# A new order of the scan's first round and of the first feed-forward splits, with chunk decays folded into ScalarE's bias columns

## The chip, the cores and the metric

One core of one Trainium2 chip runs the whole program in one launch. The metric is the device time of that core in microseconds. The engines are TensorE (PE, matmuls; PEld are its weight loads), VectorE (DVE), ScalarE (ACT), GpSimd (POOL) and the queue of SyncE (SP), which only issues loads. They run side by side and are ordered by semaphores written out by hand.

## The reference, cut to what matters

Two blocks over 256 tokens (272 in the first, which puts 16 meta tokens ahead) of width 1024, batch 1, all in float32. Block one: gated convolution and stick-breaking attention, merged and projected, then a feed-forward:

```
u, g = split(xn @ w_up_gate);  u = causal_dwconv(u, conv_w_ffn)      # width 2816
ffn = (gelu(u) * g) @ w_down
```

Block two: a layer of two scans side by side, then an attention layer. The layer of the scans, with SSD over chunks of 128 tokens and GLA (8 heads, keys of 64, values of 128) over chunks of C = 64:

```
z, xbc, dt, q, k, v, gate_lr, g = split(h @ w_in)
xs, B, C = split(silu(causal_conv(xbc)))
y = ssd_chunked_scan(xs, dt, a, B, C, d_skip);     y = rms(y * silu(z))
gcs = cumsum(log_decay within a chunk);  ref = gcs[32];  g_last = gcs[63]
scores = (q * exp(gcs - ref)) @ (k * exp(ref - gcs)),   causal
chunk_kv = (k * exp(g_last - gcs)) @ v;  the state is carried from chunk to chunk
o = scores @ v + (q * exp(gcs)) @ state;   o = rms(o) * silu(g)
out = concat(y, o) @ w_out
```

## The kernel before, in words

**Weights.** The host lays all weight matrices out as one stream of chunks, [128, 1024] each, in the order in which TensorE uses them. SyncE loads a chunk into one of four raw buffers. To multiply float32 with three fast passes, each chunk is split: ScalarE writes the rounded high half (`split_hi`, L559, `weights_hi`) and VectorE the rest (`split_lo`, L1063, `weights_lo`). Both rings hold four chunks. `feed(tile)` on either engine splits the chunk that lies four chunks ahead of the tile's own, since the tile's last matmul is what frees the ring's place. A tile is named by its stage and number: fu and fg are the up and gate projections of the feed-forward; es, eb, ec, ex, ez, eg, eq, ek, ev are those of the scan layer (small, B, C, xs, z, g, q, k, v). `project` (L1749, L1752 for ev) runs a tile: 24 matmuls of 256 columns for one chunk, 48 for the two chunks of ev. It waits first for its bank of PSUM (the tile that used the bank before must have been taken, by `conv_in`, `z_half` and so on) and then for `lo_ready` of its chunk. For the ones that matter here: feeding fu1 makes fu3's weights, fg1 makes fg3's, fu2 makes fu4's, fg2 makes fg4's; feeding ez0 makes eg1's, eg0 makes ex3's, ex2 makes eq1's, ez1 makes ek1's, eg1 and ex3 make the two of ev1, ez2 makes eg3's. Tile fg3 uses the bank of fg1, so it waits for `ffn_out(1)`.

**The feed-forward.** For each of 22 tiles i, VectorE scales u (`ffn_up`, L1313), ScalarE makes the first tap of the convolution (`ffn_tap`, L746), VectorE the two others (`ffn_conv`, L1320, two instructions), ScalarE the gelu (`ffn_gelu`, L751), GpSimd scales it (`ffn_scale`, L443), VectorE multiplies with the gate tile (`ffn_out`, L1328), ScalarE and GpSimd split the result (`ffn_high`, L755, `ffn_low`).

**The scan layer.** Rounds p = 0 to 3 each do one pair of GLA heads and two pairs u = 2p, 2p+1 of SSD heads. TensorE's order, one round: eq, ek, ev (round 0 has them ahead of the loop), ez(u), eg(u), ex(u+2), ez(u+1), eg(u+1), ex(u+3), and between these tiles the small products: `turn_x` (L1989, a transposition of xs), `ssd_heads` (L1998), `turn_keys` (L2010, transposes the decayed keys into bank 6), `gla_scores` (L2019, bank 6), `gla_kv` (L2031), `gla_out` (L2041 and L2044, bank 6), `gla_sums` (L2050). `turn_keys(p)` may write bank 6 only when `gla_norm(p-1)` has read it (`gla_on`):

```
pe.wait_ge(S("gla_kl"), p + 1)
need(pe, "gla_on", p)
```

On VectorE: `gate_sum` (L1388) and `decay_sums` (L1400) make the cumulative log decays `gcs` of two pairs; `conv_in` (L1367), `conv_rest` (L1375, three instructions) and `z_full` (L1384) do the convolution and the silu of an ex tile; `z_half` (L1435) and `z_full` those of ez and eg; `ssd_args` (L1442), `ssd_weights` (L1394), `ssd_y` (L1447), `gate_y` (L1452) and `ssd_low` (L1456) belong to SSD; `gla_scores` (L1462), `gla_states` (L1469, L1472) and `gla_norm` (L1480, L1486) to GLA. In round 0 VectorE also multiplies e_k into `kb` (L1540, `gla_kl`) and `ka` (L1543).

On ScalarE: `decays(u)` (L857, L862), `half_tanh` (L811), `tap` (L786), `take_values` (L872), `take_keys` (L878), `ssd_high` (L883, L884), `gla_exps` (L892 to L896), `gla_squares` (L900), `gla_rms` (L908, L910, with a table load before it, L542, and another at the next tanh).

On GpSimd: `gla_args(p)` (L506, L508) subtracts the chunk's reference columns from gcs, into `ka` and `kb`; `gla_keys` (L484) and `gla_products` (L490, L494, L496) multiply the exponentials with keys and queries, the queries in four products of 64 partitions each; `ssd_weights` (L470) and `ssd_add` (L476).

The order on every engine is that of the code; an instruction that waits holds up all behind it on its engine.

## Time and profile before

| | us |
|---|---|
| median of 3 runs | 849.03 (848.57 to 850.56) |
| the profiled execution, its own time | 848.99 |
| its span, first to last instruction | 847.2 |
| TensorE busy in the span | 830.6 |
| VectorE, ScalarE, GpSimd busy | 620.8, 499.1, 132.7 |

The profile is of one execution. Busy times are sums over the span; all positions in time below count from the span's start. A timeline row gives start, duration, engine, line, operation, output and inputs, and the number of instructions merged; in brackets stands the idle time before it and what ended it. The feed-forward's tiles start at about 302, the scan layer at about 496 us, and its first round ends at about 552.

### The profile page before, as it was taken

To read this page: it belongs to the slowest core of one execution; us is meant where nothing else is said; L and a number is where in the kernel's file an instruction comes from. 1 tells how busy PE (TensorE), PEld (TensorE's weight loads), DVE (VectorE), ACT (ScalarE), POOL (GpSimd) and SP (SyncE) were. 2 spreads that over 40 slices of the span, in tenths; PEclk is the share of its full clock that TensorE was granted. 3 is DMA by queue.
4 is the path that set the end of the run, shared out by engine and by line. 5 is a ranking of instruction groups with operands and counts; after the bars stand their busy time and mean duration, and the time that the engine had idled before them with its cause. 6 is when DMAs were issued, how large, how long until landed. Compare 5 with 4: busy or idle time off the path is not lost.

```text
span 847.2 us, 16833 instructions
## 1 busy us (share of the span) xinstructions
PE 830.6 (98%) x6770; PEld 800.5 (94%) x6770; DVE 620.8 (73%) x1044; ACT 499.1 (59%) x842; POOL 132.7 (16%) x131
## 2 busy tenths in 40 slices
PE   8999999999999999999999999889999999999997
PEld 7999999999999999999999999779999999888896
DVE  6547888886666688667664488997887697568764
ACT  7346657555454576555554469668768555346655
POOL 1000000000000305433441100332534011000002
PEclk9999999999999999999999999999999999999999
DMA  8754434346555536656566535455454375554431
GB/s 326 233 153 139 152 106 173 127 137 179 183 188 186 173 106 191 201 177 186 189 197 196 180 100 171 142 170 167 150 167 157 112 231 183 186 169 141 126 101 50
DMA packets 39565, 139.81 MB, mean 165 GB/s; under 512 B 4400, under 2 KB 5056, under 8 KB 39360
## 3 DMA queue, kind: packets, MB, share of 16 engines
q1 hardware_dynamic: 37728, 135.78, 50.1%
q10 hardware_dynamic: 1760, 2.96, 1.1%
q8 instruction: 54, 0.88, 0.4%
q14 instruction: 23, 0.19, 0.1%
HBM read 137.65 MB, written 1.06 MB: 164 GB/s over the span
## 4 chain that ended last, share of the span: by engine, by line
PE 90%; DVE 5%; ACT 2%; DMA 1%; issue 1%; SPq 0%; DVEq 0%; ACTq 0%
PE ps L1749 71%; PE ps L1777 5%; PE ps L1752 5%; DVE weights_lo L1063 1%; PE ps L1870 1%; PE ps L1855 1%; PE ps L1884 1%; PE ps L2127 1%; PE ps L2145 1%; PE ps L1998 1%; DMA hidden<-xT_in 1%; PE ps L2135 1%; DVE arena L1375 1%; PE ps L2041 0%; PE ps L2050 0%
## 5 line engine op out<-in xcount | busy, mean ns | idle before, releaser
L1749 PE MATMUL ps<-x_hi,weights_hi 128*128 128x256 f32 (+3 forms) x1288 | 373.0, 290 | 5.4 <-DVE weights_lo L1063 3.0
L1063 DVE TENSOR_TENSOR weights_lo<-raw_weights,weights_hi 128x1024 fp32r<-128x1024 f32 x251 | 311.5, 1245 | 85.4 <-ACT weights_hi L559 85.3
L1749 PE MATMUL ps<-x_lo,weights_hi 128*128 128x256 f32 (+3 forms) x1288 | 363.8, 282 | 0.0
L1749 PE MATMUL ps<-x_hi,weights_lo 128*128 128x256 f32 (+3 forms) x1288 | 363.2, 282 | 0.0
L559 ACT ACTIVATE weights_hi<-raw_weights 128x1024 fp32r<-128x1024 f32 x251 | 263.8, 1053 | 152.8 <-PE ps L1749 62.2
L1749 PEld LDWEIGHTS ps<-x_hi,weights_hi 128*128 128x128 f32 x1288 | 242.9, 189 | 13.6 <-issue 10.9
L1749 PEld LDWEIGHTS ps<-x_lo,weights_hi 128*128 128x128 f32 x1288 | 242.9, 189 | 1.0 <-issue 0.7
L1749 PEld LDWEIGHTS ps<-x_hi,weights_lo 128*128 128x128 f32 x1288 | 243.4, 189 | 0.0
L1749 PE MATMUL ps<-y_hi,weights_hi 128*128 128x256 f32 (+1 forms) x488 | 137.7, 282 | 0.0
L1749 PE MATMUL ps<-y_lo,weights_hi 128*128 128x256 f32 (+1 forms) x488 | 137.4, 282 | 0.0
L1749 PE MATMUL ps<-y_hi,weights_lo 128*128 128x256 f32 (+1 forms) x488 | 137.1, 281 | 0.0
L435 POOL TENSOR_TENSOR arena<-arena 128x256 f32<-128x256 f32 (+1 forms) x24 | 25.9, 1078 | 494.8 <-ACT arena L708 328.2
L1749 PEld LDWEIGHTS ps<-y_hi,weights_hi 128*128 128x128 f32 x488 | 92.0, 189 | 0.3 <-issue 0.2
L1749 PEld LDWEIGHTS ps<-y_lo,weights_hi 128*128 128x128 f32 x488 | 91.9, 188 | 0.3 <-issue 0.2
L1749 PEld LDWEIGHTS ps<-y_hi,weights_lo 128*128 128x128 f32 x488 | 92.0, 189 | 0.0
L443 POOL TENSOR_TENSOR arena<-arena,rinv 128x256 f32<-128x256 f32 x22 | 32.9, 1496 | 81.6 <-ACT arena L751 81.4
L1752 PE MATMUL ps<-weights_hi,x_hi 128*128 128x256 f32 (+1 forms) x96 | 31.0, 323 | 0.0
L1752 PE MATMUL ps<-weights_lo,x_hi 128*128 128x256 f32 (+1 forms) x96 | 30.6, 319 | 0.0
L1752 PE MATMUL ps<-weights_hi,x_lo 128*128 128x256 f32 (+1 forms) x96 | 30.6, 318 | 0.0
L746 ACT ACTIVATE arena<-arena,params 128x256 f32<-128x256 f32 x22 | 11.1, 510 | 30.2 <-DVE arena L1313 30.2
L1313 DVE TENSOR_TENSOR arena<-ps,rinv 128x258 f32<-128x258 f32 x22 | 9.4, 428 | 25.1 <-PE ps L1749 24.5
L1320 DVE SCALAR_TENSOR_TENSOR arena<-arena,params 128x256 f32<-128x256 f32 x44 | 21.9, 498 | 4.2 <-ACT arena L746 1.0
(265 smaller groups left out, 1049.6 us busy)
## 6 DMA issues: line engine op xcount, KB each, us to landing
raw_weights<-weights_in SPq DMA_DIRECT2D x252, 512.0 KB, 3.7
arena<-decay_rows ACTq DMA_DIRECT2D x8, 256.0 KB, 3.6
masks<-masks_in SPq DMA_DIRECT2D x1, 1186.0 KB, 8.3
hidden<-xT_in SPq DMA_DIRECT2D x2, 272.0 KB, 4.1
hidden<-xT_in SPq DMA_DIRECT2D x1, 544.0 KB, 5.6
raw_weights<-weights_in SPq DMA_DIRECT2D x2, 256.0 KB, 4.0
gate_w<-gate_w_in ACTq DMA_DIRECT2D x1, 256.0 KB, 5.7
out<-arena ACTq DMA_DIRECT2D x1, 256.0 KB, 2.1
```

Source lines behind the costliest of these rows:

```text
L435: ins = nc.gpsimd.tensor_tensor(sq[:, 0, t0:T], sq[:, 0, t0:T], sq[:, i, t0:T], ALU.add)
L443: g.sig(nc.gpsimd.tensor_tensor(fgl[:, i % 2, :], fgl[:, i % 2, :], rinv[:, META:T], ALU.mult), "gelu_scaled")
L559: a.sig(A(whi[:, s * CW:(s + 1) * CW], raw[:, (c % RAW) * CW:(c % RAW + 1) * CW], ACT.Copy), "hi_ready")
L746: a.sig(A(fcv[:, i % 2, :], fu[:, i % 2, 0:L], ACT.Copy, scale=pcol("conv_ffn", i)), "tap_ready")
L1063: d.sig(TT(wlo[:, s * CW:(s + 1) * CW], raw[:, (c % RAW) * CW:(c % RAW + 1) * CW], whi[:, s * CW:(s + 1) * CW].bitcast(F32), ALU.subtract) ...
L1313: d.sig(TT(fu[:, i % 2, :], r, rinv[:, TA:T], ALU.mult), "u_ready")
L1320: ins = STT(out=c_, in0=u[:, j:L + j], scalar=pcol("conv_ffn", FT * j + i), in1=c_, op0=ALU.mult, op1=ALU.add)
L1375: ins = STT(out=dst, in0=scr2[:, n % 2, j:L + j], scalar=pcol("even_conv", 10 * j + ct), in1=dst, op0=ALU.mult, op1=ALU.add)
L1749: ins = mm(bank(BANK_OF[no])[:, 0:b - a], wt, x_[:, kt, a:b], start=s0, stop=s1)
L1752: ins = mm(bank(BANK_OF[no + o])[0:t1 - t0, 0:step * P], x_[:, kt, t0:t1], wt, start=s0, stop=s1)
L1777: ins = mm(bank(BANK_OF[no])[:, 0:b - a], w_[:, at:at + P], x_[:, kt, a:b], start=kt == 0 and n == 0 and len(passes) == 2, stop=kt == KT - ...
L1855: ins = mm(bank(4 + e)[:, c0:c0 + T - t0], keysT[rows, p, k0:k0 + P], qpair[rows, p % 2, t0:T], start=n == 0, stop=n == 2, skip_group_chec ...
```

## The change: what it does

1. **GLA decays.** `gla_args` is gone from GpSimd. `decay_sums(n)` on VectorE adds three small products that put -gcs[63]/16, -gcs[32]/16 and gcs[32]/16 of each chunk into a new tile `decay_cols` and signals `gla_bias`. ScalarE's `gla_exps(p)` now reads gcs itself and takes these as bias columns: 12 activations of 64 columns and one of 256, in place of four of 256.
2. **Round 0 and the head of round 1.** ScalarE, VectorE and TensorE get a written-out order. On TensorE, gla_scores(0) moves from behind ex3 to behind eq1, ssd_heads(1) and turn_keys(0) from ahead of ex3 to behind it, gla_kv(0) behind ek1, gla_out(0) behind ev1 and ssd_heads(2), gla_sums(0) behind ez2. On VectorE the feeds come earlier and `gate_y(0)`, `gate_y(1)`, `ssd_low(0)`, `ssd_low(1)` later. `HALF` numbers the tanh buffers in the new order. The first pair's four half-height query products stay on GpSimd, which now counts VectorE's earlier signals (`g.n.update`), so that its own waits are for its own instructions.
3. **Feed-forward.** VectorE splits the chunk of fu1 between `ffn_conv(0)` and `ffn_conv(1)`, that of fg1 ahead of `ffn_out(1)`, that of fu2 ahead of `ffn_conv(2)`; ScalarE splits that of fu2 ahead of `ffn_tap(2)`.

The stream of tiles, the banks and the rings are as before. The diff, cut to its core:

```diff
+        decay_cols = sb("decay_columns", 48)[:].rearrange("p (k i c) -> p k i c", k=3, i=4)
...
-        HALF = {t: n for n, t in enumerate((s_, i_) for s_, i_, b_, n_ in STREAM if s_ in ("eb", "ec", "ex", "ez", "eg"))}
+        FIRST_HALF = [("eb", 0), ("ec", 0), ("ex", 0), ("ex", 1), ("ex", 2), ("ez", 0), ("eg", 0), ("ex", 3), ("ez", 1),
+                      ("eg", 1)]
+        HALF = {t: n for n, t in enumerate(FIRST_HALF + [(s_, i_) for s_, i_, b_, n_ in STREAM
+                                                         if s_ in ("ex", "ez", "eg") and (s_, i_) not in FIRST_HALF])}
...
             pool.wait_ge(S("cb_taken"), 2)
+            g.n.update(gla_kl=1, m_ready=4)
+            pool.wait_ge(S("gla_exp"), 1)
+            gla_products(0)
+            for p in range(1, 4):
+                ssd_weights(2 * p)
+                gla_keys(p)
+                gla_products(p)
+                ssd_add(2 * p - 1)
+                ssd_weights(2 * p + 1)
+                ssd_add(2 * p)
...
             for i in range(2, FT):
-                ffn_tap(i)
+                if i > 2:
+                    ffn_tap(i)
                 feed(("fu", i))
+                if i == 2:
+                    ffn_tap(i)
                 ffn_gelu(i)
...
             def gla_exps(p):
-                act.wait_ge(S("gla_arg"), p + 1)
+                act.wait_ge(S("gla_bias"), p // 2 + 1)
                 need(act, "gla_qk", p)
+                need(act, "sc_ready", p - 1)
                 need(act, "st_ready", p - 1)
-                a.step(A(em, ka[:, k, :], ACT.Exp, scale=-1.0 / 16))
-                a.step(A(kb[:, k, :], kb[:, k, :], ACT.Exp, scale=-1.0 / 16))
-                a.settle()
-                a.step(A(ka[:, k, :], ka[:, k, :], ACT.Exp, scale=1.0 / 16))
+                for n, (dst, scale) in enumerate(((kb[:, k, :], 1.0 / 16), (ka[:, k, :], 1.0 / 16), (em, -1.0 / 16))):
+                    for c in range(4):
+                        w_ = slice(64 * c, 64 * c + 64)
+                        a.step(A(dst[:, w_], gcs[:, p, w_], ACT.Exp, scale=scale, bias=decay_cols[:, n, p, c:c + 1]))
...
             decays(0)
+            take_values(0)
+            feed(("ez", 0))
+            half_tanh(("ex", 1), xs[:, 1, :])
+            feed(("eg", 0))
+            decays(1)
+            feed(("ex", 2))
+            gla_exps(0)
+            feed(("ez", 1))
+            tap(("ex", 2), 2, xs[:, 2, :])
+            take_keys(0)
+            feed(("eg", 1))
+            half_tanh(("ex", 2), xs[:, 2, :])
+            feed(("ex", 3))
+            half_tanh(("ez", 0), zs[:, 0, :])
+            act.wait_ge(S("xsilu"), 5)
+            half_tanh(("eg", 0), gs[:, 0, :])
+            decays(2)
+            tap(("ex", 3), 3, xs[:, 3, :])
+            feed(("eq", 1))
+            for p in range(1, 4):
+                feed(("ek", p))
+                if p == 1:
+                    gla_exps(1)
+                    take_values(1)
+                    feed(("ev", 1))
+                    half_tanh(("ex", 3), xs[:, 3, :])
+                    gla_squares(0)
+                    half_tanh(("ez", 1), zs[:, 1, :])
+                    act.wait_ge(S("xsilu"), 6)
+                    half_tanh(("eg", 1), gs[:, 1, :])
+                    ssd_high(0)
+                    decays(3)
+                    ssd_high(1)
+                    gla_rms(0)
+                    feed(("ez", 2))
+                    half_tanh(("ez", 2), zs[:, 0, :])
...
             ffn_up(0)
             ffn_up(1)
             ffn_conv(0)
+            feed(("fu", 1))
             ffn_conv(1)
-            feed(("fu", 1))
             ffn_out(0)
+            feed(("fg", 1))
             ffn_out(1)
-            feed(("fg", 1))
             for i in range(2, FT):
                 ffn_up(i)
                 if i > 2:
                     feed(("fg", i - 1))
+                else:
+                    feed(("fu", i))
                 ffn_conv(i)
                 if i > 2:
                     ffn_out(i - 1)
-                feed(("fu", i))
+                    feed(("fu", i))
...
+                at = gcs[:, 2 * n:2 * n + 2, :].rearrange("p i (c t) -> p i c t", t=64)
+                for k, (t, scale) in enumerate(((63, -1.0 / 16), (32, -1.0 / 16), (32, 1.0 / 16))):
+                    ins = TS(decay_cols[:, k, 2 * n:2 * n + 2, :], at[:, :, :, t], scale, None, ALU.mult)
+                    d.sig(ins, "gla_bias") if k == 2 else d.step(ins)
...
+            ssd_args(0)
+            ssd_weights(0)
+            split_lo()
+            z_full(("ex", 1), xs[:, 1, :], name="xsilu")
+            z_half(("ez", 0), zs[:, 0, :])
+            feed(("ez", 0))
+            ssd_y(0)
+            gate_sum()
+            decay_sums(0)
+            feed(("eg", 0))
+            z_half(("eg", 0), gs[:, 0, :])
+            ssd_weights(1)
+            ssd_args(1)
+            conv_in(("ex", 2))
+            feed(("ex", 2))
+            first_products()
+            z_half(("ez", 1), zs[:, 1, :])
+            feed(("ez", 1))
+            conv_rest(("ex", 2), 2, xs[:, 2, :])
+            ssd_y(1)
+            z_half(("eg", 1), gs[:, 1, :])
+            gla_scores(0)
+            z_full(("ex", 2), xs[:, 2, :], name="xsilu")
+            feed(("eg", 1))
+            conv_in(("ex", 3))
+            ssd_args(2)
+            gla_states(0)
+            feed(("ex", 3))
+            for p in range(1, 4):
+                take_queries(p)
+                if p == 1:
+                    take_keys(1)
+                    gate_both(0)
+                    feed(("eq", 1))
+                    conv_rest(("ex", 3), 3, xs[:, 3, :])
+                    ssd_y(2)
+                    feed(("ek", 1))
+                    z_full(("ex", 3), xs[:, 3, :], name="xsilu")
+                    gate_both(1)
+                    feed(("ev", 1))
+                    z_half(("ez", 2), zs[:, 0, :])
+                    ssd_args(3)
+                    ssd_low(0)
+                    feed(("ez", 2))
+                    ssd_low(1)
+                    gla_norm(0)
...
+                if p == 1:
+                    project(("eq", 1), xhi, xlo, META, T)
+                    gla_scores(0)
+                    project(("ek", 1), xhi, xlo, META, T)
+                    turn_x(2)
+                    gla_kv(0)
+                    project(("ev", 1), xhi, xlo, META, T, toks=toksL)
+                    ssd_heads(2)
+                    gla_out(0)
...
                 project(("ez", u), xhi, xlo, META, T)
+                if p == 1:
+                    gla_sums(0)
...
                 project(("eg", u + 1), xhi, xlo, META, T)
-                if p == 0:
-                    turn_keys(0)
-                    ssd_heads(1)
-                else:
+                if p:
                     gla_scores(p)
                 if p < 3:
                     project(("ex", u + 3), xhi, xlo, META, T)
                 if p == 0:
-                    gla_scores(0)
+                    ssd_heads(1)
+                    turn_keys(0)
```

`first_products()` is the pair of products into `kb` and `ka` (after a wait for `gla_exp`), and `gate_both(u)` is z_full of ez(u), z_full of eg(u) and gate_y(u).

## Rows read from the trace of the kernel before

**Rows 1.** Part 1 of the page: busy us, share of the span, instructions.

```profile
PE 830.6 (98%) x6770; PEld 800.5 (94%) x6770; DVE 620.8 (73%) x1044; ACT 499.1 (59%) x842; POOL 132.7 (16%) x131
```

**Rows 2.** Table of stretches: busy us (instructions) of PE, PEld, DVE, ACT, POOL, clock, DMA.

```profile
532.00:570.50 38.50, 32.95 (x260) 29.75 (x258) 35.74 (x57) 23.54 (x47) 12.45 (x13) 0.96 0.48 152
```

**Rows 3.** Waits in 495 to 575 us: in total, times, longest.

```profile
PE ps L1749 <- DVE weights_lo L1063: 2.4, 1, 2.4
PE ps L2041 <- DVE arena L1472: 2.4, 1, 2.4
```

**Rows 4.** Table of stretches, TensorE alone: busy us (instructions), granted clock.

```profile
539.00:542.00 3.00, 0.48 (x3) 1.00 0.03 10
...
543.40:546.80 3.40, 3.40 (x18) 0.50 0.46 153
...
559.00:562.00 3.00, 0.60 (x5) 1.00 0.39 152
562.00:565.00 3.00, 3.00 (x28) 1.00 0.44 105
```

**Rows 5.** Timeline of TensorE, 576 to 577 us.

```profile
576.69 0.38 PE L2010 MATMUL ps<-masks,arena 128*128 128x128 f32 x2
```

**Rows 6.** Timeline of VectorE, first round.

```profile
534.21 1.22 DVE L1063 TENSOR_TENSOR weights_lo<-raw_weights,weights_hi 128x1024 fp32r<-128x1024 f32 x1
...
543.72 1.75 DVE L1063 TENSOR_TENSOR weights_lo<-raw_weights,weights_hi 128x1024 fp32r<-128x1024 f32 x1
...
549.97 1.53 DVE L1375 SCALAR_TENSOR_TENSOR arena<-arena,params 128x256 f32<-128x256 f32 x3
...
574.21 0.87 DVE L1480 SCALAR_TENSOR_TENSOR arena<-ps,params,arena 128x256 f32<-128x256 f32 x2
```

**Rows 7.** Timeline of ScalarE, round 1.

```profile
566.11 0.40 ACT L892 ACTIVATE arena<-arena 128x256 f32<-128x256 f32 x1
...
567.48 1.04 ACT L559 ACTIVATE weights_hi<-raw_weights 128x1024 fp32r<-128x1024 f32 x1
...
571.02 1.28 ACT L542 ACT_TABLE_LOAD   x1
572.31 0.69 ACT L908 ACTIVATE arena<-ps,masks 128x512 f32<-128x512 f32 x1
...
576.62 1.48 ACT L857 ACTIVATE arena<-arena,dt_and_cumsum 128x256 f32<-128x256 f32 x4
578.00 0.51 ACT L862 ACTIVATE arena<-arena 128x384 f32<-128x384 f32 x1
...
578.83 1.04 ACT L559 ACTIVATE weights_hi<-raw_weights 128x1024 fp32r<-128x1024 f32 x1
```

**Rows 8.** Groups by line and shape, ScalarE, 500 to 575 us: busy, mean ns.

```profile
L857 ACT ACTIVATE arena<-arena,dt_and_cumsum 128x256 f32<-128x256 f32 x6 | 3.0, 498 | 1.2 <-DMA arena<-decay_rows 1.2
...
L857 ACT ACTIVATE arena<-arena,dt_and_cumsum 128x128 f32<-128x128 f32 x6 | 2.3, 388 | 0.0
```

**Rows 9.** Timeline of GpSimd, first products.

```profile
543.58 0.80 POOL L494 TENSOR_TENSOR arena<-arena 64x256 f32<-64x256 f32 x1
544.46 1.60 POOL L496 TENSOR_TENSOR arena<-arena 64x256 f32<-64x256 f32 x1
```

**Rows 10.** Timeline of all engines, start of the feed-forward.

```profile
317.53 1.05 ACT L559 ACTIVATE weights_hi<-raw_weights 128x1024 fp32r<-128x1024 f32 x1
...
319.30 1.76 DVE L1063 TENSOR_TENSOR weights_lo<-raw_weights,weights_hi 128x1024 fp32r<-128x1024 f32 x1
...
321.20 0.35 PE L1749 MATMUL ps<-x_hi,weights_hi 128*128 128x258 f32 x1 [0.56 <-DVE weights_lo L1063]
...
324.15 0.28 PE L1749 MATMUL ps<-x_hi,weights_hi 128*128 128x256 f32 x1
...
327.53 1.22 DVE L1063 TENSOR_TENSOR weights_lo<-raw_weights,weights_hi 128x1024 fp32r<-128x1024 f32 x1
...
330.14 0.28 PE L1749 MATMUL ps<-x_hi,weights_hi 128*128 128x256 f32 x1
```

102 lines of the change are left out of this document (23 added, 79 removed).

## Prediction, made before the changed kernel was run

> **What bounds the kernel now.** I read the page's busy times first. TensorE is busy for 830.6 of 847.2 us, VectorE for 620.8 and ScalarE for 499.1 [rows 1]; so only time in which TensorE waits, or runs at a lower clock, can be won, some 16 us in all. The table of stretches then says where the edited scan stands: in 532.0 to 570.5 us TensorE is busy 32.95 of 38.5 us and VectorE 35.74 [rows 2]. There VectorE is the bound, not TensorE. The waits of that stretch name two stops of 2.4 us each: the first matmul of tile eg1 waits for `weights_lo` (L1063), and `gla_out(0)` (L2041) waits for the last carry of `gla_states(0)` (L1472) [rows 3]. The same table with TensorE alone shows a third loss: after the first stop the granted clock is 0.50 for 3.4 us (543.4 to 546.8) and 18 matmuls run in it, where 3.0 us at 1.00 hold 28 [rows 4]. At 0.118 us a matmul, 18 need 2.1 us; so 1.3 us are lost. After the second stop the clock stays at 1.00. These three, 2.4 + 2.4 + 1.3, and a few tenths at other edges make 7 us: the most that a new order of the first round can give. In the feed-forward only 0.56 us are idle, before fu3 at 321.20 [rows 10].
>
> **The feed-forward.** VectorE now splits the fu1 chunk (feeding tile fu3) between the two first convolutions. ScalarE's high half comes at 318.6 (317.53 + 1.05), GpSimd is still idle, so VectorE is done at 318.6 + 1.2 = 319.8; today it ends at 319.30 + 1.76 = 321.06 [rows 10]. fu3 then follows fu2 without a wait: 0.7 us won (idle and the pipeline's fill). But work queues behind it. `ffn_conv(1)` ends at 321.35 (2 x 0.5, and GpSimd's first scale holds the port for 0.6). ScalarE stands in `ffn_gelu(1)` until then, so its high half of fg1 is ready at 321.8 + 1.0 = 322.7, and VectorE's low half at 324.0; `ffn_out(1)`, now behind it, ends at 324.3 and frees fg3's bank: fg3 starts at 324.45, where it starts at 324.15 now. Then `ffn_up(2)` 324.8, high half of fu2 325.7 (behind `ffn_high(1)`), low half 326.95, and only then `ffn_conv(2)` to 328.0, gelu 328.4, high half of fg2 329.4, low half 330.65. Today that low half starts at 327.53 and ends at 328.75, and tile fg4 starts at 330.14 with 1.4 us to spare [rows 10]. With the change fg4 starts at 330.75, 0.6 late, and fg5 waits up to 0.4 more for `ffn_out(3)`. After that VectorE has about 0.9 us a tile to spare and catches up, while TensorE, which has no idle time there, gives nothing back. I take +0.8 us; bounds -0.7 (nothing but the gain) and +1.3.
>
> **The scan up to the second tile of round 1.** VectorE's pieces: a low half takes 1.22 us (1.13 to the next start), a three-step convolution 1.53 [rows 6]. With `z_full(ex1)` ahead of `z_half(ez0)`, and feed(ez0) ahead of gate_sum, the low half for eg1 is ready at 537.4, not 541.9; eg1 starts at 539.1, right after turn_x(1), and the stop and the low clock there are gone. gate_sum, two scans, a settle and three tiny TENSOR_SCALARs end at 540.7 (no 128x8 row exists; 128x4 and 128x50 ones take 0.17 and 0.18, 0.1 apart, so 0.3 for three).
>
> The exponentials then cost more on ScalarE. Today four take 566.11 to 567.48, 1.37 us [rows 7]. Now twelve of 64 columns with a bias column, and one of 256, are issued. With a bias column, two of 256 columns and two of 128 take 1.38 us from 576.62 to the next start [rows 7]; their durations differ by 0.11 [rows 8], so they cost 0.40 and 0.29 each. The 0.11 for 128 columns makes 0.235 for 64: 12 x 0.235 + 0.32 = 3.1 us, 1.8 more per pair (bounds 0.1 each, 1.5 in all, and 0.29 each, 3.8). In return GpSimd loses its two subtractions per pair. The Trainium skill, "ScalarE: Activation LUTs", section "What ACT_TABLE_LOAD costs", gives 280 ns + 0.833 ns a column with a pointer bias and 93 ns of overlap; by it the twelve would make 2.9 us, an estimate.
>
> So `gla_exp` comes at 544.0 (541.9 today). GpSimd's four half-height products are the ones it does today; one takes 0.80 us with the port nearly free and 1.60 behind a VectorE pass, and the pass beside them takes 1.75 instead of 1.22 [rows 6, 9]. Letting the two alternate (operands in PSUM don't collide), they end at 548.8, VectorE's product for `gla_kl` at 547.0 and `ka` at 548.4. turn_keys(0) waits 0.9 us for the former; behind it queue eq1 (547.3), gla_scores(0) and ek1 (550.9). turn_x(2) and gla_kv(0) follow at 553.8, ev1 at 555.2 (behind `conv_in(ex3)`, which frees its bank), to 561.1. The states are ready at 556.4, so gla_out(0), now behind ssd_heads(2), waits for nothing. ez2 runs 563.5 to 566.4, then gla_sums(0), turn_x(3), and eg2 to 570.3. In the trace eg2's end is turn_keys(1) at 576.69 [rows 5]. The lead is 6.4 us.
>
> **What is late next: turn_keys(1).** It overwrites bank 6 and so waits for `gla_norm(0)` (`gla_on`). Today that sits at 574.21 and is done at 575.1, 1.6 us ahead of its reader [rows 5, 6]. In the new order more stands before it on both engines. ScalarE: gla_exps(1) 558.5 to 561.6, take_values(1) 562.3, two high halves 564.2, tanh ex3, squares, tanh ez1 565.3, wait for `xsilu` 6 at 566.1 (VectorE's convolution and feed alternate with GpSimd's six products of pair 1), tanh eg1 566.5, ssd_high(0) 0.8, decays(3) 2.2 (576.62 to 578.83 in the trace), ssd_high(1) 0.8, table load 1.3, Ln and Exp 1.3: 573.0 [rows 7]. Then feed(ez2) is ahead of gla_norm(0) on VectorE: high half 1.05, low half 1.15, ssd_low(1) 0.4, gla_norm 0.9: `gla_on` at 576.5, turn_keys(1) at 576.6. Against 576.69: -0.1 us. The whole lead becomes one wait of about 6.2 us. Bounds: VectorE's own work cannot bring it before 573.6 (-3.1, ScalarE never late); the dearer activation, twice in this chain, makes it 577.9 (+1.2).
>
> The row puts a table load at 1.29 us to the next start (571.02 to 572.31) [rows 7]. The same section of the Trainium skill's "ScalarE: Activation LUTs" adds a drain of 1.38 us to each load; by it turn_keys(1) would come at about 577.9, an estimate. The trace shows only some 0.1 us of it, and the sum goes by the trace.
>
> **The clock.** An idle stretch of 2.4 us, with little else around it, was followed by 3.4 us at 0.50; the other 2.4 us stop was not [rows 4]. A wait of 6.2 us is far beyond both, so I expect the lower level (1.2 GHz) when ex4 starts. One such stretch costs 1.3 us, two in a row 2.6; I take 1.7 (bounds 0 and 2.6). The Trainium skill, "TensorE: Matmul & The Clock Gate", section "What's actually happening", says the same of an idle array: its clock is halved until work comes; the trace agrees (0.50).
>
> Later rounds: pairs 2 and 3 pay 1.8 us more of ScalarE before gla_norm(p-1), which has 1.5 us of slack, but GpSimd starts its decay products earlier without gla_args, and that returns about a microsecond. I cost it at 0.1, and it goes into the rounding.
>
> **The sum**, against the profiled execution, 848.99 us around a span of 847.2 (median of the runs 849.03, the same): +0.8 - 0.1 + 1.7 = +2.4, so 851.4 us.
>
> **Rivals.**
> - *The wait stands, the clock holds.* For it: one of two stops left the clock alone. Against: this one is 2.6 times as long. 848.99 + 0.8 - 0.1 = 849.7. Chance 0.10.
> - *The ScalarE chain is shorter than I make it*, and turn_keys(1) is bound by VectorE alone near 574: the gain of 3.1 stays, the clock hardly falls, 846.7 (with the feed-forward's gain too 845.2). For it: VectorE has idle time in my walk only while it waits for ScalarE's high half of ez2. Against: six steps of this chain are priced by rows. Chance 0.14, 0.09 of it below 846.5.
> - *Slower: the 64-column activations cost what 128 columns cost*, 0.29 each. Then turn_keys(1) is at 577.9, the wait 7.5 us, and the clock stays low for two stretches: 848.99 + 0.8 + 1.2 + 2.6 = 853.6. It decides from 0.25 us an activation on. Chance 0.14.
>
> **Chances and range.** The forecast itself, 849.8 to 853.0, has 0.62. Within 0.3% (2.5 us, about what this measurement can tell from no change) means 846.5 to 851.6; the forecast lies at its upper edge and gives 0.28 above it. Slower: 0.28 + 0.13 = 0.41; faster 0.09; same 0.50. The range that leaves 2 in 10 out is 847.4 to 853.3.
>
> **What would show it.** Right: no wait at eg1 or at gla_out(0); low halves ready before fu3 but fg4 some 0.6 us late; eg2 ending near 570; then a wait of 5 to 7 us at turn_keys(1) (L2010 of before) ended by VectorE's gla_norm, and granted clock 0.50 behind it. Wrong: turn_keys(1) before 575, or a granted clock of 1.00 after it, or 64-column activations outside 0.19 to 0.29 us, or TensorE idle elsewhere in round 1.

## The result, and the profile after

The changed kernel takes 851.01 us (median of 18 runs, 850.07 to 852.00); the kernel before, on the same chip, 849.33 us (18 runs, 848.57 to 851.15). The recorded ratio is 1.0013, 95% interval 1.0007 to 1.0019: 0.13% slower, within the 0.3% that was called no change (the medians alone differ by 1.68 us, 0.20%). The profiled execution took 850.85 us around a span of 849.2, where before's took 848.99 around 847.2. Before's 18 runs on this chip fall into two groups with nothing between 849.49 and 850.26 us: ten around 849.0 and eight around 850.5. Its profile is one of the lower group. So the difference of the two profiles, 1.86 us, is near the largest that the runs show; counted from the upper group the change costs 0.5 us.

Part 1 of the page of the changed kernel, against [rows 1]: ScalarE works 6.4 us more, GpSimd 7.9 us less, TensorE 1.6 us more although its 6770 instructions are the same.

```profile
PE 832.2 (98%) x6770; PEld 802.0 (94%) x6770; DVE 621.9 (73%) x1050; ACT 505.5 (60%) x878; POOL 124.8 (15%) x123
```

The scan starts 0.7 us later than before, so the stretch that answers to [rows 2] is 532.7 to 571.2 us. In the table of stretches TensorE is busy for 37.02 us of 38.5 (32.95 before), at clock 1.00 (0.96 before), and does 309 matmuls (260 before):

```profile
532.70:571.20 38.50, 37.02 (x309) 34.21 (x307) 36.70 (x60) 30.78 (x74) 13.78 (x13) 1.00 0.57 168
```

So round 0 became what it was to become. The waits in 532 to 577 us, TensorE's lines, against [rows 3]: the two stops of 2.4 us are gone and one of 5.4 us has come.

```profile
PE ps L2059 <- DVE arena L1494: 5.4, 1, 5.4
...
PE ps L2059 <- DVE arena L1525: 0.6, 1, 0.6
```

L2059 is `turn_keys`, L1494 `gla_norm`; the 0.6 us are turn_keys(0)'s, for which 0.9 were forecast. TensorE's timeline (against [rows 5], 576.69) and the table of stretches with TensorE alone (against [rows 4]) show the wait and what follows it: 5.3 us without a matmul, then 4.8 us at clock 0.50 with 23 matmuls, then 31 matmuls in 3.4 us at 1.00. The mean of 0.81 over the wait means that the last 2.0 us of it were at 0.50 already, so the low level lasted 6.8 us in all.

```profile
575.95 0.66 PE L2059 MATMUL ps<-masks,arena 128*128 128x128 f32 x2 [5.37 <-DVE arena L1494]
```

```profile
570.60:575.90 5.30, 0.00 (x0) 0.81 0.63 209
575.90:580.70 4.80, 4.75 (x23) 0.50 0.52 170
580.70:584.10 3.40, 3.40 (x31) 1.00 0.12 48
```

The chain that ends in L1494, on ScalarE and then VectorE (timelines of both, against [rows 6, 7]). Four decay activations and two exponentials of decays(3) stand in it, then the table load, Ln, Exp and a high half; on VectorE the low half of that chunk and `ssd_low(1)` are still ahead of `gla_norm(0)`.

```profile
565.71 0.42 ACT L799 ACTIVATE arena<-arena 128x256 f32<-128x256 f32 x1 [0.16 <-DVE arena L1394]
...
566.74 1.48 ACT L845 ACTIVATE arena<-arena,dt_and_cumsum 128x256 f32<-128x256 f32 x4
...
569.77 1.28 ACT L527 ACT_TABLE_LOAD   x1
571.07 0.69 ACT L897 ACTIVATE arena<-ps,masks 128x512 f32<-128x512 f32 x1
...
572.33 1.04 ACT L544 ACTIVATE weights_hi<-raw_weights 128x1024 fp32r<-128x1024 f32 x1
```

```profile
573.40 1.23 DVE L1071 TENSOR_TENSOR weights_lo<-raw_weights,weights_hi 128x1024 fp32r<-128x1024 f32 x1 [0.81 <-ACT weights_hi L544]
574.54 0.48 DVE L1470 SCALAR_TENSOR_TENSOR y_lo<-arena,params,y_hi 128x256 fp32r<-128x256 f32 x1
574.93 0.87 DVE L1494 SCALAR_TENSOR_TENSOR arena<-ps,params,arena 128x256 f32<-128x256 f32 x2
```

In the feed-forward the waits in 300 to 340 us answer to [rows 10]. The first is that ahead of fg3 (for `ffn_out(1)`, L1336), the second that ahead of fg4 (for its low half, L1071); the 0.56 us ahead of fu3 are gone.

```profile
PE ps L1798 <- DVE arena L1336: 0.8, 1, 0.8
PE ps L1798 <- DVE weights_lo L1071: 0.6, 1, 0.6
```

Round 3 has a loss that the prediction had put at 0.1 us and rounded away. ScalarE does its twelve exponentials (2.97 us) ahead of the two high halves of ev3; VectorE stands 2.24 us for those, so `ssd_y(6)` (L1461) comes at 645.03, and turn_x(7) on TensorE waits 0.39 us for it (timelines of the three engines):

```profile
637.47 2.97 ACT L884 ACTIVATE arena<-arena,decay_columns 128x64 f32<-128x64 f32 x12
...
640.65 1.99 ACT L544 ACTIVATE weights_hi<-raw_weights 128x1024 fp32r<-128x1024 f32 x2
...
641.73 3.39 DVE L1071 TENSOR_TENSOR weights_lo<-raw_weights,weights_hi 128x1024 fp32r<-128x1024 f32 x2 [2.24 <-ACT weights_hi L544]
645.03 0.47 DVE L1461 SCALAR_TENSOR_TENSOR arena<-arena,params,ps 128x256 f32<-128x256 f32 x1
...
645.65 0.41 PE L2038 MATMUL ps<-masks,arena 128*128 128x128 f32 x2 [0.39 <-DVE arena L1461]
```

To compare kernels whose lines and clocks of start differ, I take differences between the starts of the same matmuls in each profiled timeline: F is the feed-forward's first matmul to the scan section's first; the others count from the latter, to turn_keys(1), turn_x(5), turn_x(7) and the first matmul of the output projection. What follows that is 186.1 us in all of them. What stands ahead of F differs by up to 1.4 us between the profiled executions (the first matmul of F comes at 301.72 to 303.13) and is no part of any edit. The latest of them is that of early states, the one profile in which the granted clock fell back to 0.50 early in the kernel (10.9 to 14.3 us), so its own time says nothing about its edit. A difference in F below 0.3 us says nothing either: the eight kernels with the change's lines in the feed-forward have 194.45 to 194.75.

| us | F | keys(1) | x(5) | x(7) | output |
|---|---|---|---|---|---|
| before | 193.74 | 80.84 | 113.06 | 148.06 | 159.43 |
| changed | 194.75 | 79.38 | 113.51 | 149.08 | 160.61 |
| old feed-forward order | 193.75 | 79.36 | 112.81 | 148.38 | 159.92 |
| feed-forward part alone | 194.74 | 82.40 | 114.59 | 149.60 | 160.92 |
| work in the wait | 194.71 | 79.38 | 111.38 | 146.95 | 158.48 |
| early normalisation | 194.71 | 74.94 | 111.01 | 146.61 | 158.14 |
| high halves first | 193.36 | 79.41 | 112.81 | 148.38 | 159.95 |
| early states | 194.53 | 74.97 | 111.06 | 146.62 | 158.14 |
| round 3 | 194.45 | 79.40 | 113.47 | 148.49 | 162.82 |
| four moves | 193.43 | 74.95 | 111.08 | 146.14 | 160.43 |
| exponentials ahead | 194.69 | 74.94 | 108.75 | 143.85 | 155.36 |
| the same, high halves first | 193.44 | 75.00 | 108.80 | 143.90 | 155.42 |
| decay columns alone | 193.69 | 81.64 | 115.19 | 150.43 | 161.92 |
| products on VectorE | 194.51 | 79.37 | 113.00 | 148.57 | 160.10 |

The first two rows are the whole account: +1.01 in the feed-forward; -1.46 up to turn_keys(1); +1.91 from there to turn_x(5), which holds the low clock; +0.57 from turn_x(5) to turn_x(7); +0.16 after; -0.29 ahead of F, which no edit touches. Together +1.90, and the last matmul of the changed kernel ends 1.90 us later (843.32 for 841.42).

### The profile page after: what moved, and what is told of

Read it like the earlier page. It is cut to its first block, busy times and chain, and to the rows that moved or that the text cites. A ratio compares the mean times of both kernels' runs of the same rounds, so it can differ in the third digit from the quotient of the medians.

```text
span 849.2 us, 16867 instructions
## 1 busy us (share of the span) xinstructions
PE 832.2 (98%) x6770; PEld 802.0 (94%) x6770; DVE 621.9 (73%) x1050; ACT 505.5 (60%) x878; POOL 124.8 (15%) x123
## 4 chain that ended last, share of the span: by engine, by line
PE 86%; DVE 6%; ACT 4%; issue 2%; DMA 1%; POOL 0%; SPq 0%; DVEq 0%; ACTq 0%; POOLq 0%
PE ps L1798 69%; PE ps L1826 5%; PE ps L1801 4%; DVE weights_lo L1071 2%; ACT weights_hi L544 1%; PE ps L1919 1%; PE ps L1904 1%; PE ps L1933 1%; PE ps L2185 1%; PE ps L2203 1%; DVE arena L1385 1%; DMA hidden<-xT_in 1%; PE ps L2193 1%; PE ps L2047 0%; ACT arena L845 0%
## 5 line engine op out<-in xcount | busy, mean ns | idle before, releaser
L1071 DVE TENSOR_TENSOR weights_lo<-raw_weights,weights_hi 128x1024 fp32r<-128x1024 f32 x251 | 311.9, 1247 | 91.4 <-ACT weights_hi L544 91.3
```

The costliest lines, as they stand in the source:

```text
L1071: d.sig(TT(wlo[:, s * CW:(s + 1) * CW], raw[:, (c % RAW) * CW:(c % RAW + 1) * CW], whi[:, s * CW:(s + 1) * CW].bitcast(F32), ALU.subtract) ...
```

## The experiments

Each ratio is the recorded one, to runs of the kernel before on the same chip. The medians of before were 850.29 us (35 runs) for experiments 1 to 4, 849.94 (29) for 5 to 8 and 850.47 (21) for 9 to 12, so a time below must not be set against the 849.33 above. No kernel here differs from before by as much as 2%; the intervals say which differences are clear of noise.

**1. Old feed-forward order.** The changed kernel, with before's place for the fu1 and fg1 low halves on VectorE and the tap of round 2 on ScalarE.

```
-            feed(("fu", 1))
             ffn_conv(1)
+            feed(("fu", 1))
             ffn_out(0)
-            feed(("fg", 1))
             ffn_out(1)
+            feed(("fg", 1))
```

> The changed kernel with the feed-forward's splits put back into the old order; the scan keeps the change. My theory: the feed-forward part costs 1.0 us (fg4 starts late and nothing gives it back), so this comes out 1.0 us below the changed kernel, about +0.5 us against the kernel before; the stretch from the first feed-forward tile to the first scan tile is 193.7 us again (194.75 in the changed kernel). Rival: the feed-forward part is hidden or neutral and all of the difference is the scan's; then this equals the changed kernel, +1.5 us.

849.68 us (11 runs), ratio to before 0.9997 (0.9988 to 1.0005), the same as before within the interval. F goes back to 193.75 from 194.75.

**2. The feed-forward part alone.** The same lines the other way round, in the kernel before.

> The kernel before with only the feed-forward part of the change. My theory: +1.0 us against the kernel before (850.3), tile fu3 starting without a wait and fg4 and fg5 late. Rival, that the earlier split pays as it is meant to: -0.7 us (848.6).

851.36 us (12 runs), ratio 1.0011 (1.0002 to 1.0020). F is 194.74: the edit costs 1.00 us wherever it stands. That the two experiments agree to 0.01 is partly luck: over all profiles with these lines F is 0.7 to 1.0 us above before's. But this scan, which is before's to the letter, is 1.5 us longer. Both stops of 2.4 us are there as in [rows 3]; this time the granted clock also fell behind the second. The table of stretches has 19 matmuls in 3.7 us where [rows 4] have 28 in 3.0:

```profile
562.60:566.30 3.70, 3.70 (x19) 0.54 0.42 130
```

So whether a 2.4 us stop costs clock differs between executions of one order, and 1.5 us of a single profile's difference can be that. The runs of the kernel before say the same. For 85 of them the mean granted clock is on record. Of the 45 with 0.996 or more, 34 took 849.51 us or less; the 40 with 0.995 or less took 849.94 or more, all of them. The two groups of the result lie at the same times; their clocks are not on record.

**3. Work in the wait.** The changed kernel, with nine matmuls into the unused sums bank ahead of turn_keys(1); nothing reads them. The timeline has them as 18 instructions, 4.05 us together.

```
             def turn_keys(p):
+                if p == 1:
+                    for _ in range(9):
+                        mm(bank(SSB)[:, 0:L], ones, mask("ones"), start=True, stop=True)
                 pe.wait_ge(S("gla_kl"), p + 1)
```

> The changed kernel with nine matmuls of the ones mask (0.54 us each by the five that the kernel already uses this way) put into the wait at turn_keys(1), writing a bank nobody reads. My theory: the clock's fall is a cost of its own; the granted clock stays at 1.00 behind the wait, ex4 and ez3 take 5.8 us and not 7.8, and the kernel is 2.1 us below the changed one, about -0.5 us against the kernel before. Rival, that the low clock is hidden because VectorE and ScalarE bound that stretch anyway: the same as the changed kernel, or slower by what the matmuls push turn_keys(1) back (under 0.3 us).

849.10 us (11 runs), ratio 0.9991 (0.9983 to 1.0000). Its table of stretches, TensorE alone:

```profile
571.00:576.50 5.50, 4.05 (x20) 1.00 0.69 212
576.50:580.50 4.00, 3.96 (x34) 1.00 0.49 138
```

turn_keys(1) comes at the same time (79.38), but the clock stays at 1.00, and turn_x(5) is at 111.38 instead of 113.51: the low clock cost 2.13 us. In experiment 1, whose scan has the same order and the same wait of 5.4 us, the low stretch was 3.4 us instead of 6.8 and turn_x(5) at 112.81: 1.43 us. Its table of stretches, TensorE alone:

```profile
575.20:578.40 3.20, 3.16 (x15) 0.50 0.41 150
```

So the rival, a low clock hidden behind VectorE and ScalarE, falls.

**4. Early normalisation.** The two moves that put the chain to gla_norm(0) ahead of work that nobody waits for.

```
                     half_tanh(("eg", 1), gs[:, 1, :])
+                    gla_rms(0)
                     ssd_high(0)
                     decays(3)
                     ssd_high(1)
-                    gla_rms(0)
...
                     feed(("ev", 1))
+                    gla_norm(0)
                     z_half(("ez", 2), zs[:, 0, :])
...
                     ssd_low(1)
-                    gla_norm(0)
```

> The changed kernel with gla_rms(0) moved ahead of ssd_high(0), decays(3), ssd_high(1) on ScalarE, and gla_norm(0) ahead of z_half(ez2), ssd_args(3), ssd_low and feed(ez2) on VectorE. My theory: the lead of the new first round is real and is swallowed by that chain alone; turn_keys(1) comes 4.2 us earlier, the wait before it falls to about 1.1 us, the clock stays at 1.00: 6 us below the changed kernel, about -4.5 us against the kernel before. Rival: another wait stands right behind (decay weights for ssd_heads(3), the split chunk of eg3) and takes the time back: within 1 us of the changed kernel.

849.26 us (12 runs), ratio 0.9991 (0.9981 to 1.0001). turn_keys(1) comes 4.44 us earlier (74.94) and the clock stays at 1.00, worth 2.13 more by experiment 3; yet at turn_x(5) only 2.50 us are left of the 6.57. The 6 us that I had expected were wrong; the rival, another wait right behind, was right in kind, though the wait is at neither of the two places that it names and a part of the gain stayed. TensorE's waits in 566 to 612 us, and VectorE's timeline:

```profile
PE ps L2090 <- DVE arena L1486: 3.2, 1, 3.2
PE ps L2059 <- DVE arena L1494: 0.9, 1, 0.9
PE ps L2038 <- DVE arena L1461: 0.5, 1, 0.5
```

```profile
591.67 1.27 DVE L1410 TENSOR_TENSOR_SCAN arena<-masks,arena 128x256 f32<-128x256 f32 x2
592.97 0.32 DVE L1414 TENSOR_SCALAR decay_columns<-arena 128x8 f32<-128x8 f32 x3
593.40 0.42 DVE L1377 TENSOR_TENSOR arena<-ps,rinv 128x256 f32<-128x256 f32 x1
...
594.05 0.73 DVE L1486 SCALAR_TENSOR_TENSOR arena<-arena,ps 128x128 f32<-128x128 f32 x2
```

gla_out(1) (L2090) now waits 3.2 us for gla_states(1) (L1486), which stands behind decay_sums(1) (L1410, L1414) and the start of ex5's convolution. In the changed kernel TensorE got there at 598.1 us, after the states (ready at 596.7), and no wait showed.

**5. High halves first.** The changed kernel, with ScalarE's high halves of the fg1 and fg2 chunks ahead of the gelus of tiles 1 and 2.

```
             ffn_gelu(0)
-            ffn_gelu(1)
             feed(("fg", 1))
+            ffn_gelu(1)
...
                     ffn_tap(i)
+                    feed(("fg", i))
                 ffn_gelu(i)
                 if i > 2:
                     ffn_high(i - 1)
-                feed(("fg", i))
+                    feed(("fg", i))
```

> The change with one more move in the feed-forward: ScalarE's high halves of the fg1 and fg2 chunks come ahead of gelu(1) and gelu(2). Theory (the queue behind the convolution makes fg3 and fg4 late): TensorE's waits of 0.8 us before fg3 and 0.5 us before fg4 go, the first feed-forward tile to the first scan tile takes 193.3 to 193.7 us where the change takes 194.75, and the span is about 1.3 us under the change's 849.2. Rival (VectorE itself is too late there, the order on ScalarE does not matter): both waits stay within 0.2 us of 0.8 and 0.5. The scan is untouched: turn_keys(1) waits 5.3 us and the granted clock falls behind it in both.

850.15 us (11 runs), ratio 1.0004 (0.9995 to 1.0013). F is 193.36, 1.39 less than with the change and 0.38 less than before (193.43 and 193.44 in experiments 8 and 10). Of the two waits that ahead of fg4 is gone, and of that ahead of fg3 0.4 us are left:

```profile
PE ps L1799 <- DVE arena L1337: 0.4, 1, 0.4
```

**6. Early states.** Experiment 4, and gla_states(1) moved up to right behind feed(eg3) on VectorE.

```
                 feed(("eg", u + 1))
+                if p == 1:
+                    gla_states(1)
                 z_full(("ez", u + 1), zs[:, 1, :])
```

> The early normalisation as before (rms and gla_norm of pair 0 ahead of ssd_high, decays(3) and z_half(ez2)), and gla_states(1) moved on VectorE from behind decay_sums(1) to right behind the low half of eg3. Theory (removing the first wait moved the limit to the states of pair 1, which stand behind four passes, a scan pair and a convolution's start): the wait of 3.2 us at gla_out(1) goes, the states end near 591.1 instead of 594.8, TensorE keeps clock 1.00, and the span is 2.5 to 3.2 us under that of early normalisation alone (846.7), so 843.5 to 844.2. Rival (VectorE as a whole is the bound of rounds 1 and 2, each pass moved ahead makes another late): the sum of TensorE's waits between 570 and 620 us stays near 4.5 us and the span near 846.5.

849.36 us (11 runs), ratio 0.9991 (0.9980 to 1.0001). The wait at gla_out(1) is gone, and nothing is won: turn_x(5) is at 111.06, where experiment 4 had 111.01. TensorE's waits in 566 to 612 us:

```profile
PE ps L2041 <- DVE arena L1461: 2.0, 1, 2.0
PE ps L1804 <- issue: 1.7, 1, 1.7
```

Both new ones were always next in line. ev2 (L1804) overwrites the bank that ex5's convolution start frees, and that stands behind decay_sums(1) (its end and ev2's start agree to 0.1 us; the row names no releaser). turn_x(5) waits for ssd_y(4) (L1461), which stands behind two low halves, whose high halves ScalarE makes only after the twelve exponentials of pair 2. My expectation for this kernel, 2.5 to 3.2 us less, was wrong. The waits of TensorE between 566 and 612 us still sum to 4.6 us, as in experiment 4, which is what the rival said (VectorE as a whole is the bound); experiment 9, with turn_x(5) at 108.75, decides against it.

**7. Round 3.** The changed kernel, with `feed(("ev", 3))` ahead of `gla_exps(3)` on ScalarE.

```
                     gla_squares(p - 1)
+                    if p == 3:
+                        feed(("ev", p))
                     gla_exps(p)
-                    feed(("ev", p))
+                    if p < 3:
+                        feed(("ev", p))
```

> The change with one move: in round 3 ScalarE makes the high halves of ev3 ahead of the twelve exponentials of pair 3. Theory (the 0.5 us that round 3 loses against before come from the exponentials standing in front of the ev3 halves, so VectorE idles 2.2 us and ssd_y(6) is late): the wait before turn_x(7) goes, the scan from the first round to its end is 0.4 to 0.6 us shorter than the change's 175.39 us. Rival (the exponentials then make GpSimd's products and turn_keys(3) late): a new wait at turn_keys(3) or gla_scores(3) of about the same size, no gain.

853.34 us (5 runs), ratio 1.0043 (1.0031 to 1.0055): the slowest of all. turn_x(5) to turn_x(7) falls from 35.57 to 35.02 us (before 35.00), so the cause of the 0.57 us is the exponentials' place. But from there to the output projection it takes 14.33 us for 11.53. Waits of TensorE in 575 to 665 us, and ScalarE's timeline:

```profile
PE ps L2062 <- DVE arena L1497: 6.4, 2, 5.4
PE ps L2050 <- POOL arena L474: 1.6, 2, 1.4
```

```profile
640.68 1.06 ACT L544 ACTIVATE weights_hi<-raw_weights 128x1024 fp32r<-128x1024 f32 x1 [1.79 <-DVE weights_lo L1074]
641.65 2.96 ACT L884 ACTIVATE arena<-arena,decay_columns 128x64 f32<-128x64 f32 x12
```

The second high half of ev3 has to wait 1.79 us until VectorE (L1074) is done with the buffer that it overwrites, and the exponentials wait behind it: they start at 641.65, where the changed kernel has them at 637.47. So they are 4.2 us late, not the 1.9 us of two high halves. All that follows on ScalarE is late with them. The table load and gla_rms(2) make gla_norm(2) late (L1497, 1.0 us of waiting for turn_keys(3)), and decays(7) makes GpSimd's weights late (L474, 1.4 us for ssd_heads(7)): GpSimd is done with its products and idles 2.21 us for decays(7) ahead of L474.

**8. Four moves.** Experiments 4 to 7 together.

> All moves together: early normalisation, gla_states(1) earlier, high halves ahead of the gelus, ev3 halves ahead of the exponentials. If the four losses are separate they add: against the change's span of 849.2, -6.6 (wait and clock at turn_keys(1)) +0.4 (small waits that come back) -1.3 -0.5, so 841 us. If they share one limit (VectorE), it ends near 845.

851.12 us (12 runs), ratio 1.0016 (1.0007 to 1.0025). Column for column it is experiment 6 up to turn_x(5), experiment 5 in F, and experiment 7 behind turn_x(7) (14.29 us). My 841 us of span assumed separate losses, and 845 if they shared a limit; it is 848.5. Neither was right, since one of the four moves costs time.

**9. Exponentials ahead.** Experiment 6, with the exponentials of pairs 2 and 3 moved to the end of the round before, where ScalarE is idle, and the start of ex5's convolution ahead of decay_sums(1).

```
                     feed(("eq", p + 1))
+                    gla_exps(p + 1)
                     half_tanh(("ex", u + 3), xs[:, u + 3, :])
...
                     gla_squares(p - 1)
-                    gla_exps(p)
                     feed(("ev", p))
...
+                if p < 3:
+                    conv_in(("ex", u + 3))
                 if p == 1:
                     decay_sums(1)
-                if p < 3:
-                    conv_in(("ex", u + 3))
```

> Early normalisation and early states as before, and for pairs 2 and 3 ScalarE's exponentials go from behind the squares into the end of the round before, behind the high half fed by eq(p+1), where ScalarE is idle for 2 to 3 us; VectorE does the start of ex5's convolution ahead of the two scans of decay_sums(1) instead of behind them. Theory (what early normalisation gains is stopped in turn by single passes that stand in the wrong place: the bank of ev2 by ex5's start, turn_x(5) by the high halves behind the exponentials): the waits of 1.7 us at ev2 and 2.0 us at turn_x(5) go, round 3 loses nothing at ssd_y(6), and first scan tile to turn_x(7) takes 142.5 to 143.5 us where the change takes 149.1 and early normalisation 146.6. Rival (VectorE's total work is the bound there): TensorE's waits between 570 and 650 us still sum to over 3 us, and the stretch stays above 145.5.

845.65 us (5 runs, 845.54 to 845.93), ratio 0.9948 (0.9935 to 0.9960). Scan to turn_x(7) takes 143.85 us, 5.2 less than with the change (142.5 to 143.5 were expected). The waits of TensorE that are left in rounds 1 to 3 sum to 2.1 us, so the rival (VectorE's total work is the bound, over 3 us of waits left) falls. What each of the three moves is worth by itself was not tried.

**10. The same, high halves first.** Experiments 9 and 5.

> The same with the high halves ahead of gelu(1) and gelu(2) in the feed-forward. Theory: the feed-forward gives its 1.4 us as it did alone (first tile to first scan tile 193.4 us), the scan as in the run before it: 841 to 843 us of span, some 0.7% under the kernel before. Rival: as above, near 845.5.

844.75 us (5 runs, 844.45 to 845.25), ratio 0.9937 (0.9925 to 0.9950): 0.63% faster than before, the fastest kernel here (0.7% was expected). TensorE's waits in 566 to 665 us are three:

```profile
PE ps L2063 <- DVE arena L1495: 0.9, 1, 0.9
PE ps L2051 <- DVE arena L1457: 0.7, 1, 0.7
PE ps L2042 <- DVE arena L1462: 0.5, 1, 0.5
```

In the table of stretches TensorE is busy for 34.67 of 36.0 us and VectorE for 34.05. All three waits that are left are for passes of VectorE, so VectorE is the next limit there, but little is left to win: 2.1 us.

```profile
571.00:607.00 36.00, 34.67 (x289) 32.46 (x288) 34.05 (x59) 29.30 (x58) 13.32 (x12) 1.00 0.57 179
```

**11. Decay columns alone.** The kernel before with the twelve exponentials, the three small passes on VectorE and no subtractions on GpSimd; the order is before's.

```
-                a.step(A(em, ka[:, k, :], ACT.Exp, scale=-1.0 / 16))
-                a.step(A(kb[:, k, :], kb[:, k, :], ACT.Exp, scale=-1.0 / 16))
-                a.settle()
-                a.step(A(ka[:, k, :], ka[:, k, :], ACT.Exp, scale=1.0 / 16))
+                for n, (dst, scale) in enumerate(((kb[:, k, :], 1.0 / 16), (ka[:, k, :], 1.0 / 16), (em, -1.0 / 16))):
+                    for c in range(4):
+                        w_ = slice(64 * c, 64 * c + 64)
+                        a.step(A(dst[:, w_], gcs[:, p, w_], ACT.Exp, scale=scale, bias=decay_cols[:, n, p, c:c + 1]))
```

> The kernel before with only the decay columns: twelve exponentials of 64 columns with a bias instead of three of 256, three small passes more on VectorE and GpSimd's subtractions gone; no order is changed. Theory (the columns cost 1.7 us of ScalarE a pair, which before has slack in rounds 1 and 2 but not in round 3): the scan is 0.3 to 0.8 us longer, with a small wait before turn_x(7), and the wait at gla_out(0) grows from 2.4 by up to 1.5 us. Rival (GpSimd's part returned pays for it): within 0.3 us of before's 174.2 us of scan.

851.16 us (11 runs), ratio 1.0012 (1.0003 to 1.0021). The scan is 2.49 us longer, more than I had expected (0.3 to 0.8): 0.80 of it up to turn_keys(1), 1.33 from there to turn_x(5), 0.24 to turn_x(7) and 0.12 after. The wait at gla_out(0) did not grow (2.4), and the expected one before turn_x(7) is not there. Waits of TensorE in 532 to 665 us:

```profile
PE ps L2031 <- DVE arena L1462: 3.2, 2, 2.4
PE ps L1739 <- DVE weights_lo L1049: 1.7, 1, 1.7
PE ps L2009 <- ACT arena L863: 1.3, 1, 1.3
PE ps L1979 <- DVE arena L1437: 1.2, 3, 0.5
```

Up to turn_keys(1), the stop at eg1 is 0.7 us shorter than before's and a wait of 1.3 us at gla_scores(0), for the turned keys of pair 0 (L863), is new. Behind it, the additions are a second wait at gla_out, 0.8 us in round 1, and 0.3 us at turn_x(5).

**12. Products on VectorE.** The changed kernel, with the first pair's four half height query products behind `ka` on VectorE.

```
-            gla_products(0)
...
+                for e in range(2):
+                    rows = slice(64 * e, 64 * e + 64)
+                    d.step(TT(qg[rows, 0, e, :], eg[rows, 0, :], e_q[rows, 0, :], ALU.mult))
+                    ins = TT(qe[rows, 0, e, :], em[rows], e_q[rows, 0, :], ALU.mult)
+                    d.sig(ins, "gla_qk") if e else d.step(ins)
```

> The change with the four half height query products of the first pair on VectorE, behind ka, instead of on GpSimd. Theory (in round 0 of the changed kernel VectorE's time has room, since all of it drains into the wait at turn_keys(1), which ScalarE's chain sets): the product for gla_kl takes 0.42 us instead of 0.94, turn_keys(0) waits 0.1 us or not at all instead of 0.6, and turn_keys(1) comes within 0.6 us of the change's; the span within 0.7 us of 849.2. Rival (VectorE is the bound of round 0 and pays 4 x 0.34 us): convolution and xsilu 6 are 1 us or more later, so that turn_keys(1) is 1 us later and the span about 850.3.

850.91 us (11 runs), ratio 1.0007 (0.9998 to 1.0016). turn_keys(1) is at 79.37, as with the change. VectorE's timeline, first of the changed kernel, where GpSimd has the four products, then of this one (its first row is the product for `gla_kl`, the second the last of the four):

```profile
544.93 1.70 DVE L1071 TENSOR_TENSOR weights_lo<-raw_weights,weights_hi 128x1024 fp32r<-128x1024 f32 x1
546.55 0.94 DVE L1525 TENSOR_TENSOR arena<-arena 128x256 f32<-128x256 f32 x1
...
548.47 0.42 DVE L1449 SCALAR_TENSOR_TENSOR arena<-ps,rinv 128x256 f32<-128x256 f32 x1
```

```profile
545.77 0.42 DVE L1523 TENSOR_TENSOR arena<-arena 128x256 f32<-128x256 f32 x1
...
547.56 0.42 DVE L1528 TENSOR_TENSOR arena<-arena 64x256 f32<-64x256 f32 x1
548.08 0.42 DVE L1447 SCALAR_TENSOR_TENSOR arena<-ps,rinv 128x256 f32<-128x256 f32 x1
```

Counted from the scan's first matmul, the pass behind the products starts at 51.90 us with GpSimd's help and at 51.85 without it: VectorE does four passes more in the same time, because GpSimd's cost it about as much in waiting: 0.48 us at the low half (1.70 for 1.22) and 0.52 or 0.53 at each of the two products (0.94 and 0.95 for 0.42), 1.5 us in all. The rival, that VectorE pays for the four passes, falls. The wait at turn_keys(0) went, but one of 0.6 us at ev1 came, for the convolution's start that these passes are ahead of.

## Why the prediction was right, step by step

The total was forecast as +2.4 on 848.99 and the profiled execution shows +1.86; the median, 851.0, is 0.4 us from the 851.4. The mechanism is the one forecast: the stops of round 0 go, their time becomes one wait at turn_keys(1), the clock falls behind it, and the feed-forward loses. That the total is so close is partly luck, since the misses offset each other: +0.2 in the feed-forward, -1.4 up to turn_keys(1), +0.2 from there to turn_x(5), where the low clock lies, +0.7 in the later rounds, and -0.3 ahead of F, which is no part of the change.

- **Feed-forward, +0.8:** measured 1.01, and 1.00 by experiments 1 and 2. The mechanism is the stated one (the queue behind ffn_conv(1)): fu3 comes 0.7 us earlier, as forecast, and fg3 and fg4 are the late tiles. Counted from the feed-forward's first matmul, fg3 starts 0.2 us later than before (0.3 forecast) and fg4 0.7 (0.6); the last 0.3 come behind it (up to 0.4 were allowed for). Experiment 5 shows that it was in the main ScalarE's order, not VectorE's work, that made them late: with the high halves first the wait ahead of fg4 goes and that ahead of fg3 is halved.
- **The stops go and their time becomes one wait:** right. No wait at eg1 and none at gla_out(0); eg2 ends at 570.6, which is 569.9 in before's time (its scan starts 0.73 earlier), for 570.3 predicted; the wait is 5.4 us for 6.2. Experiment 4 shows that this wait, and nothing else, held turn_keys(1): with the chain moved up it comes 4.4 us earlier. The lower bound of the forecast, 573.6, is for VectorE's order as it stood, and no run tests it with ScalarE on time; experiment 4, which changes that order too, has turn_keys(1) at 570.8 in before's time.
- **Scan up to turn_keys(1), -0.1:** this step was mis-sized, it measured -1.46. From tanh(eg1) on the walk is good: 10.4 us were forecast up to gla_norm's end and 10.1 are seen. It is the start that was late in the walk: 566.1 forecast, 565.0 seen (565.71 less 0.73). 0.6 us of that stood already at ev1 (555.2 for 554.65), the rest is in the passes beside GpSimd's products of pair 1, which I let take turns all the way. In the timeline, ex3's convolution takes 1.88 us and the low half behind it 1.36, against 1.53 and 1.22 alone.

```profile
561.24 1.88 DVE L1385 SCALAR_TENSOR_TENSOR arena<-arena,params 128x256 f32<-128x256 f32 x3
...
563.44 1.36 DVE L1071 TENSOR_TENSOR weights_lo<-raw_weights,weights_hi 128x1024 fp32r<-128x1024 f32 x1
```

- **The dearer exponentials, 0.235 us each:** right. The groups by shape of ScalarE in 532 to 577 us have them at 334 ns, and the twelve take 2.97 us, 0.24 to the next start. The rival at 0.29 falls.

```profile
L884 ACT ACTIVATE arena<-arena,decay_columns 128x64 f32<-128x64 f32 x24 | 5.9, 334 | 2.7 <-DVE decay_columns L1414 2.7
```

- **The clock, +1.7 (0 to 2.6):** the mechanism is shown by experiment 3. It cost 2.13 us in this execution, 1.43 in one with the shorter low stretch. The rival in which it holds falls for each of the five profiled executions that had the 5.4 us wait without work in it (the changed kernel, experiments 1, 5, 7 and 12). The low level did not end when work came: 4.8 us of it, with 23 matmuls, lie behind the wait. That the sum took 848.99 for before, an execution of the lower group, was not said; against the upper group the clock's price is partly in before as well.
- **Later rounds, 0.1:** this was wrong in size and in kind. From turn_x(5) to turn_x(7) 0.57 us are lost, and 0.16 more behind that, whose cause stays open. I had weighed only gla_norm(p-1) behind the dearer exponentials; what they delay is the pair of high halves behind them, and through VectorE ssd_y(6). Experiments 7 and 9 show it: the first removes 0.55 of the 0.57 us at a price elsewhere, the second 0.47 without one. The columns alone cost 2.49 us in before's order (experiment 11), and the changed scan is only 1.18 us longer than before's with a low stretch twice as long in it as in the profiles of those two (6.8 us for 3.4). So the new order hid most of their price, as far as single profiles tell.
- **The rival with the shorter chain** described where the -1.46 came from, but not its end: turn_keys(1) came at 575.2 in before's time, not near 574, ScalarE's chain was still the bound (VectorE idles 0.81 us for the high half of ez2), and the clock fell all the same.

The change's parts, as the runs have them: the new order of round 0 wins its stops back, is stopped at one wait, loses 1.4 to 2.1 us to the clock behind it, and the feed-forward adds up to 1 us. What remained is 1.1 us in 849 by the ratio and 1.9 by the two profiles.

## What to carry to other kernels

When an edit removes waits, follow each engine's queue to the next shared buffer and ask what stands ahead of the pass that frees it: here 5 us went into one normalisation that stood behind work nobody waited for. Removing that wait let single passes stop TensorE one after the other (3.2, 1.7, 2.0 us), and only moving all of them paid: 0.52%, and 0.63% with the feed-forward's order. A pass moved behind a dearer one is a pass moved later; the exponentials were harmless where ScalarE idled and cost 2.2 us net of the scan where they were postponed behind a pass that itself had to wait.

## What the runs showed of the hardware

- The granted clock after an idle stretch is not the same in every execution: the same 2.4 us stop was followed by 3.4 us at 0.50 in one and by none in another; behind the 5.4 us wait it was 3.4 us (experiment 1) or 6.8 us (the changed kernel). In each the low level ran on while TensorE was working again; behind the 5.4 us wait it cost 1.4 to 2.1 us. Nine matmuls that nothing reads, 4.05 us of work in the wait, kept it at 1.00 in the profiled execution, and 1.5 us of idle time were left in it.
- GpSimd's four half height products beside VectorE cost VectorE about as much as doing them itself: 0.94 us for a pass of 0.42, 1.70 for one of 1.22. The Trainium skill, "SBUF — State Buffer", section "Who interferes with whom", says that a VectorE pass with two SBUF inputs and a GpSimd pass that reads SBUF exclude each other, and that issue order decides who blocks. The rows here agree (the 0.94 and 0.95 us passes), and experiment 12 puts the price: 1.5 us of waiting on VectorE for four products that take it 1.6 us.
- A table load takes 1.28 us and 1.30 to the next activation's start (569.77 to 571.07; in [rows 7] 571.02 to 572.31); no drain of over a microsecond shows ahead of or behind it.
